# The first of ScalarE's three scalings moved ahead of the copies of a transformer layer's gate stage

## The reference, cut to what matters

```
eid  = take_along_axis(cand_i, pos)        # i1 * 128 + i2: 128 experts for each token
gate = softmax(top_s)
a    = gelu(h . peer_u[eid])
out  = sum over the 128 picks of (gate * a) * peer_v[eid]
```

## Time and profile before

| | |
|---|---|
| median of three runs | 966.27 us |
| profiled execution, its own time | 966.27 us |
| its span in the trace | 964.5 us |
| TensorE busy | 947.8 us, 98% of the span |
| VectorE busy | 760.8 us, 79% |
| ScalarE busy | 479.4 us, 50% |
| GpSimd busy | 206.4 us, 21% |
| granted TensorE clock | 1.00 |

### The profile page before, as it was taken

How to read it: one execution, slowest core, us unless ns; L and a number is a source line. 1 busy time by engine, 2 the same in 40 slices (tenths; PEclk the granted TensorE clock), 3 DMA queues, 4 the chain that set the end, 5 groups by cost and what they waited for, 6 DMA issues and landing times.

```text
span 964.5 us, 16295 instructions
## 1 busy us (share of the span) xinstructions
PE 947.8 (98%) x5302; PEld 824.5 (85%) x5302; DVE 760.8 (79%) x1450; ACT 479.4 (50%) x846; POOL 206.4 (21%) x252
## 2 busy tenths in 40 slices
PE   7999999999999999999999999999999999999998
PEld 7998899898888887888888888888888888888887
DVE  6898767979999988887777677777777777777766
ACT  5576545433888874334443444444434434444442
POOL 4064226977777740000000000000000000000000
PEclk9999999999999999999999999999999999999999
DMA  8544129846544458777545555555455555555554
GB/s 283 159 131 131 46 89 334 207 117 194 151 136 129 137 166 253 241 242 232 192 174 194 198 177 200 188 178 209 178 189 203 175 195 195 178 203 184 183 208 153
DMA packets 73882, 176.82 MB, mean 183 GB/s; under 512 B 6241, under 2 KB 39137, under 8 KB 73329
## 3 DMA queue, kind: packets, MB, share of 16 engines
q1 hardware_dynamic: 72976, 171.73, 52.9%
q0 software_dynamic: 576, 4.19, 2.2%
q10 hardware_dynamic: 288, 0.37, 0.1%
HBM read 165.26 MB, written 6.82 MB: 178 GB/s over the span
## 4 chain that ended last, share of the span: by engine, by line
PE 89%; DVE 5%; DMA 3%; ACT 2%; issue 0%; SPq 0%; DVEq 0%; POOLq 0%; ACTq 0%
PE psum L1888 36%; PE psum L1868 17%; PE psum L1753 12%; PE psum L1871 9%; PE psum L1516 4%; PE psum L1831 3%; PE psum L1722 3%; DMA rr<-big 2%; PE psum L1532 1%; DVE rr L831 1%; DMA big<-in_w_in_dram 1%; PE psum L1714 1%; DVE big L923 1%; PE psum L1747 1%; DVE big L949 1%; PE psum L1662 1%
## 5 line engine op out<-in xcount | busy, mean ns | idle before, releaser
L1888 PE MATMUL psum<-rr 128*128 128x512 f32 x1536 | 366.5, 391 | 0.7 <-DVE rr L1265 0.7
L1888 PEld LDWEIGHTS psum<-rr 128*128 128x128 f32 x1536 | 287.4, 188 | 61.1 <-DVE rr L1265 1.4
L1868 PE MATMUL psum<-h_all,rr 128*128 128x512 f32 x728 | 260.6, 392 | 0.0
L777 ACT ACTIVATE rr<-raw 128x1024 fp32r<-128x1024 f32 x94 | 99.7, 1061 | 240.1 <-PE psum L1888 237.7
L1233 DVE TENSOR_TENSOR rr<-raw,rr 128x1024 fp32r<-128x1024 f32 x94 | 115.2, 1225 | 125.7 <-ACT rr L777 125.7
L1871 PE MATMUL psum<-h_all,rr 128*128 128x256 f32 x728 | 188.8, 280 | 0.0
L1868 PEld LDWEIGHTS psum<-h_all,rr 128*128 128x128 f32 x728 | 136.6, 188 | 27.3 <-issue 0.4
L1871 PEld LDWEIGHTS psum<-h_all,rr 128*128 128x128 f32 x728 | 136.7, 188 | 7.1
L1753 PE MATMUL psum<-t32s,raw 128*128 128x256 f32 x576 | 131.6, 379 | 0.0
L675 ACT ACTIVATE rr<-raw 128x1024 fp32r<-128x1024 f32 x91 | 96.6, 1061 | 48.0 <-DMA raw<-in_peer_u_dram 46.6
L1753 PEld LDWEIGHTS psum<-t32s,raw 128*128 128x128 f32 x576 | 106.1, 190 | 13.2 <-issue 0.2
(11 more groups left out here) (205 smaller groups left out, 1085.2 us busy)
## 6 DMA issues: line engine op xcount, KB each, us to landing
raw<-in_peer_v_dram SPq DMA_DIRECT2D x128, 512.0 KB, 3.6
raw<-in_peer_u_dram SPq DMA_DIRECT2D x127, 512.0 KB, 4.0
big<-in_w_in_dram SPq DMA_DIRECT2D x10, 1024.0 KB, 6.1
big<-in_peer_wq_dram SPq DMA_DIRECT2D x8, 1024.0 KB, 6.1
up_kept<-gel SPq DMA_DIRECT2D x36, 128.0 KB, 1.7
gel<-up_kept SPq DMA_DIRECT2D x34, 128.0 KB, 3.5
big<-in_w_out_dram SPq DMA_DIRECT2D x4, 1024.0 KB, 5.4
rr<-big POOLq DMA_DIRECT2D x4, 1024.0 KB, 9.6
```

The lines of the kernel that those rows point to most:

```text
L777: act.activation(v_sp[s][:, 0, :], v_raw[s], ACT.Copy).then_inc(v_hi, 1)
L1868: return pe.matmul(both, ut[s][:, 0, k, :], ht[:, :, k, :], start=(k == 0), stop=(k == DK - 1))
L1888: i = pe.matmul(psum[:, 4 + 2 * t + n, :], g_sp[:, s, x, t * P:(t + 1) * P], v_sp[s][:, y, n * 512:(n + 1) * 512], start=(first and m == 0 ...
```

## The change

ScalarE takes tokens 0 to 2 of each quad, where it took 5 to 7; GpSimd takes 3 to 7, where it took 0 to 4. ScalarE now waits for the cols of quad q (and, from q = 2 on, for the products of quad q - 2) and scales token 0 before the two `keep_high` of the quad before; tokens 1 and 2 follow behind them. TensorE waits for ScalarE's part ahead of the first half, where it waited between the halves.

```diff
-            def gated(q):
+            def gated(q, first, last):
 
-                for j in range(GRP - ACT_T, GRP):
+                for j in range(first, last):
                     tok = GRP * q + j
                     for part, scale in ((0, f(p_hi(tok, 1))), (1, picks[:, 2, tok:tok + 1])):
-                        if q == 0 and part:
+                        if tok == 0 and part:
                             act.wait_ge(d_plo, 1)
                         i = act.activation(pairs_at[q % 2][:, j, part, :], cols[:, q % 2, j, :], ACT.Copy, scale=scale)
-                i.then_inc(ohg_up, 1)
+                if last == ACT_T:
+                    i.then_inc(ohg_up, 1)
...
             for q in range(NQ):
+                act.wait_ge(oh_up, 2 * q + 1)
+                if q >= 2:
+                    act.wait_ge(b_done, 2 * q - 2)
+                gated(q, 0, 1)
                 if q:
                     keep_high(2 * q - 2)
                     keep_high(2 * q - 1)
-                act.wait_ge(oh_up, 2 * q + 1)
-                gated(q)
+                gated(q, 1, ACT_T)
...
-                n, tok = GRP - ACT_T, GRP * q
+                n, tok = GRP - ACT_T, GRP * q + ACT_T
...
-                    i = pool.tensor_tensor(pairs_at[q % 2][:, 0:n, part, :], cols[:, q % 2, 0:n, :],
+                    i = pool.tensor_tensor(pairs_at[q % 2][:, ACT_T:, part, :], cols[:, q % 2, ACT_T:, :],
                                            p.unsqueeze(2).to_broadcast([P, n, NK]), ALU.mult)
...
                 pe.wait_ge(oh_up, 2 * q + 2)
+                pe.wait_ge(ohg_up, q + 1)
                 pe.wait_ge(ohp_up, q + 1)
                 gate_half(q, 0)
-                pe.wait_ge(ohg_up, q + 1)
                 gate_half(q, 1)
```

## The result

The changed kernel is slower: 973.43 us median over six runs (971.11 to 974.54) against 966.96 us for the kernel before (966.01 to 968.59, six runs), a ratio of 1.0067 with a 95% interval of 1.0051 to 1.0084. That is 6.5 us where 7.75 was forecast. The profiled execution took 973.24 us, 6.97 more than the one before, with a span of 971.4 us. The clock stayed at 1.00.

What follows compares the result with a forecast made beforehand. VectorE's own work of 3.46 us per quad was taken to bound the loop, added time passing to the kernel. 966.27 + 7.25 for the stalls + 0.5 at the end gave 974.0 us, range 971.5 to 977.0.

Steps and rivals of the forecast that it cites:

- Token 0 ahead of the copies: ScalarE's scaling starts 1.30 us after the cols, two take 0.58, so the first copy starts at 1.88 instead of 1.16.
- my lower bound of 0.20 for the stall: Least stall of VectorE per quad, from 1.29 for the release and the copy's 0.595 us without latency.
- Copy to add_low: add_low can start 0.63 us after the copy starts, at 2.51; VectorE, free at 2.27, waits 0.24 us.
- The beat: Cols to next cols: 2.51 plus 1.20 from add_low to cols, 3.71 us against 3.46, 0.25 more per quad.
- How many quads: Quads 2 to 30, 29 in all, each push the next cols by 0.25 us: 7.25 us.
- The end: Behind the last quads, the copy after TensorE's last products begins at 5.3 instead of 4.77: 0.5 us once.
- What else moves: Other engines' effects: TensorE's products start at about 4.2 instead of 3.86, covered by 0.6 us; nothing added.
- A: Rival, chance 0.07: ScalarE's release costs more or TensorE's products come late for the copies; 3.5 us more, 977.5 us.
- B: Rival, chance 0.04: the stall is given back behind the loop, by up to 5.35 us; 966 to 969 us.
- C: Rival, chance 0.02: TensorE's waits set the loop's beat, so earlier scaling gains at most 4.8 us; 961.5 us.
- D: Rival, chance 0.01: TensorE's clock falls to 1.2 GHz in the loop, +71 us, 1045 us.
- One of the signs that I named: In the timeline after, add_low shows idle time, some 7 us in total over 29 waits of about 0.24.

Runs made afterwards that it cites:

- The first experiment: The changed kernel with all six scalings behind the two copies again, token swap and TensorE's earlier wait kept; 973.80 us, ratio 1.0065 to the kernel before.
- the kernel with six rows: The kernel before with one-hot rows written for 6 of 8 tokens from quad 2 on; 963.69 us, ratio 0.9976.
- the second: The changed kernel with bf16 cols, token by column, each pick stored twice; 963.85 us, ratio 0.9965 to the kernel before.
- The first kernel with cols in pairs: The kernel before with bf16 cols, token by column, each pick stored twice so VectorE reads neighbouring pairs; 964.90 us, ratio 0.9984.

## Why the prediction was right

The direction, the place and the mechanism held; the stall of a quad was put at 0.25 us and was 0.20.

1. **Token 0 ahead of the copies.** I took 1.30 for the release and 0.58 for two scalings. In the steady loop the first scaling starts 1.25 behind the cols; 1.31 is that of quad 0 alone, in the changed kernel too (241.02 to 242.34), and the 1.29 of the earlier trace rows is GpSimd's, which is released later than ScalarE (304.24 and 304.19 for the same cols). So my lower bound of 0.20 for the stall was none, since it was built on the 1.29: add_low waited 0.19. The two scalings took 0.60. The copy came at 1.85, not 1.88.
2. **Copy to add_low.** 0.61 instead of 0.63, add_low at 2.46, not 2.51: a wait of 0.19 instead of 0.24.
3. **The beat.** Add_low to cols was 1.20 as taken. The beat is 3.66, not 3.71. This is the term that was mis-sized: the 29 quads made 5.87 us, 0.202 each, instead of 7.25. The chain was right to 0.05 in 3.71, but the stall is the small difference of two long sums, so an error of 1.4% in the chain became 20% in the stall.
4. **How many quads.** The wait starts in quad 2: cols at 248.03 and then 251.69, 3.66 later. 29 quads, as said.
5. **The end.** 0.42 us instead of 0.5. It came as counted: the last products start 4.44 behind the cols (said 4.45), but the copy followed them by 0.75, not by 0.86, at 5.19 against 4.77 before.
6. **What else moves.** TensorE's products start 4.17 behind the cols (299.28 to 303.45; said 4.2). The copy of them starts at 304.79, 1.34 later, and such a copy could start 0.75 behind the products, so 0.59 us cover TensorE's wait, as said (0.6). What I did not see is how much hangs on this cover. I wrote that without it the wait "would cost what it exceeds" and gave it no number. The first experiment has it: in the old order of ScalarE's work TensorE's wait costs the whole 6 us. So the early scaling is not the only cause that the change holds, it is one of two, and in this kernel the one that ends last. Once TensorE waits ahead of the first half, the early scaling takes two scalings out of the loop of ScalarE and TensorE (3.67 to 3.08) and puts them into that of VectorE and ScalarE (3.06 to 3.66). And I had TensorE wrong in size: I read its weight loads as 12% free and as 3.0 us of a quad. In the kernel with six rows they are busy 91% of the time (86.66 of 95 us) with no gap over 0.03 us between the groups, and TensorE's own work is 3.34 us of a quad. Its slack in the kernel before was 0.12 us. Nothing of the forecast hung on it, because the beat went up.

The forecast of 974.0 us lies 0.6 from the measured median of 973.43, and that is closer than the working deserves. The terms as measured, 5.87 and 0.42, would have made 972.6, at the lower edge of the sum's bounds. The kernel before is 0.69 us slower in the median of six runs than in the 966.27 that I started from, and that made up for part of the error.

The copy's own duration is 579 ns on the mean in the changed kernel (595 before). The Trainium skill's 612 ns ("ScalarE: Activation LUTs", section "What ACT_TABLE_LOAD costs") is above both; by it the wait would have been put higher, and it was lower.

The rivals. A (ScalarE's release costs more) is refuted, it cost less: 1.25. B (given back behind the loop) is refuted: from the first product of the next stage to the end of the span both kernels take the same, 608.5 and 608.7 us. C (faster, because TensorE's waits set the beat) is refuted: the early scaling alone made the kernel slower, and less work for VectorE made the kernel before faster. D: the clock did not fall, with up to 0.7 us of waiting before TensorE's weight loads in each quad.

One of the signs that I named was wrong in size: I expected some 7 us of idle time before add_low and the group shows 3.2. Both the idle time and the stall are real. VectorE's rows last 1.21 us but the next instruction can start 1.13 behind their start, so of a stall of 0.19 only 0.11 shows as idle. A stall is read from start to start.

What stays open: the 0.68 us outside the loop, which are less than runs of one kernel differ by; and TensorE's earlier wait without the swap of the tokens, which was not run.

## What to carry to other kernels

Before moving work ahead of something else in an engine's queue, write down each closed loop through the engines (here cols, scaling, copy, add_low, cols; and products, copies, scalings, products) with its length: the beat is the longest of them and of each engine's own work. A move takes time out of one loop and puts it into another, and it pays only while the one that it lengthens stays the shorter. Two edits that each close a loop do not add up, so undoing one of them alone can show no effect, and only changing each by itself, in both directions, tells what each would cost.

## What the runs showed of the hardware

- VectorE's is_equal with 1024 elements on each partition took 1.21 us with fp32 inputs of which one lay in PSUM, and 0.68 us with bf16 inputs and output in SBUF. Type and place changed together; no run has only one of them. It kept 0.68 when each value of one input was repeated over 64 pairs and only the two numbers of a pair lay side by side.
- ScalarE's scaling of 128 elements took 0.40 us (0.29 from start to start) from fp32 or contiguous bf16, but 0.52 (0.42) from bf16 numbers 16 bytes apart; GpSimd's with 640 elements 1.26 and 1.56. The Trainium skill, "SBUF — State Buffer", section "Door 1: The DMA port swizzle", tells of lines of 16 bytes, and that each access that crosses into a new line pays; these numbers agree in direction, and the size is theirs alone. The Trainium skill, "ScalarE: Activation LUTs", section "What ACT_TABLE_LOAD costs", has ScalarE at one rate for fp32 and bf16, and that holds here only without the stride.
- The bf16 cols in pairs lasted 1.78 us instead of 0.68 in quad 1, where GpSimd's instruction (1.25 us from 244.89) ran beside them; in the steady loop GpSimd waits for the cols and they never meet. It is so in both kernels with such cols (in the second from 244.31, beside GpSimd from 244.29). In the kernel before, the cols of quad 1, with one input in PSUM, lasted 1.22 us beside GpSimd's instruction from 243.23, so they were not slowed. These are three rows, and I made no run for it. The first kernel with cols in pairs, then the kernel before:

```profile
244.91 1.78 DVE L1223 TENSOR_TENSOR raw<-raw 128x1024 bf16<-128x1024 bf16 x1
...
243.25 1.22 DVE L1200 TENSOR_TENSOR raw<-psum,picks 128x1024 f32<-128x1024 f32 x1
```
